# Stage borders of a two-block Hyena/attention network: ScalarE rounds the next input and squares it into the bank just read

## What is computed

```python
y = x32 * lax.rsqrt(jnp.mean(x32 * x32, axis=-1, keepdims=True) + EPS)   # over the 1024 channels
return (y * g.astype(jnp.float32)).astype(x.dtype)
x = x + mixed
x = x + swiglu(rmsnorm(x, norm_ffn[i]), w_gate, w_up, w_down)
```

## Time and profile before

| | us |
|---|---|
| median of 3 runs | 2171.7 (2170.68 to 2172.7) |
| the profiled execution, its own time | 2171.51 |
| its span, first to last instruction | 2169.7 |
| PE busy with matmuls | 2035.8 (94%) |
| DVE busy | 1156.2 (53%) |
| ACT busy | 660.4 (30%) |
| POOL busy | 883.4 (41%) |
| mean granted TensorE clock | 0.941 of full |

### The profile page before, as it was taken

How to read it: one execution, slowest core, us unless ns; L and a number is a source line. 1 busy time by engine, 2 the same in 40 slices (tenths; PEclk the granted TensorE clock), 3 DMA queues, 4 the chain that set the end, 5 groups by cost and what they waited for, 6 DMA issues and landing times. The chain is left out here.

```text
span 2169.7 us, 22805 instructions
## 1 busy us (share of the span) xinstructions
PE 2035.8 (94%) x8683; PEld 1620.5 (75%) x8683; DVE 1156.2 (53%) x1404; ACT 660.4 (30%) x931; POOL 883.4 (41%) x370
## 2 busy tenths in 40 slices
PE   6887788999999999999988999999999969999999
PEld 5665677888888777556866888888787857888887
DVE  6776677544443575544847444433668566535301
ACT  3554432222222223212332322222223342222221
POOL 3465324444454434100531444454443513444442
PEclk8998899999999999657979999999999989999999
DMA  4221012333323322100321333223323303232222
GB/s 145 72 93 58 20 59 78 97 97 97 97 87 107 94 78 79 40 1 20 117 78 39 97 97 97 94 90 97 101 89 116 117 20 96 93 99 92 96 92 73
DMA packets 167194, 179.32 MB, mean 83 GB/s; under 512 B 4511, under 2 KB 156563, under 8 KB 166868
## 3 DMA queue, kind: packets, MB, share of 16 engines
q1 hardware_dynamic: 164036, 172.16, 24.8%
q10 hardware_dynamic: 3088, 6.20, 0.8%
HBM read 176.24 MB, written 2.10 MB: 82 GB/s over the span
## 5 line engine op out<-in xcount | busy, mean ns | idle before, releaser
L1849 POOL TENSOR_TENSOR w_lo<-w_raw,w_hi 128x1024 fp32r<-128x1024 f32 x326 | 817.2, 2527 | 1166.2 <-ACT w_hi L1477 1166.2
L490 PE MATMUL acc<-a_hi,w_hi 128*128 128x512 f32 x1544 | 610.7, 396 | 25.3 <-POOL w_lo L1849 10.9
L491 PE MATMUL acc<-a_lo,w_hi 128*128 128x512 f32 x1544 | 604.7, 392 | 0.0
L492 PE MATMUL acc<-a_hi,w_lo 128*128 128x512 f32 x1544 | 604.4, 391 | 0.0
L1477 ACT ACTIVATE w_hi<-w_raw 128x1024 fp32r<-128x1024 f32 x326 | 327.1, 1051 | 541.9 <-PE acc L492 537.7
L490 PEld LDWEIGHTS acc<-a_hi,w_hi 128*128 128x128 f32 x1544 | 291.8, 189 | 101.0 <-issue 16.0
L491 PEld LDWEIGHTS acc<-a_lo,w_hi 128*128 128x128 f32 x1544 | 291.8, 189 | 62.2 <-issue 1.7
L492 PEld LDWEIGHTS acc<-a_hi,w_lo 128*128 128x128 f32 x1544 | 291.5, 189 | 62.4
L490 PE MATMUL acc<-h_hi,w_hi 128*128 128x512 f32 x528 | 205.4, 389 | 0.0
L491 PE MATMUL acc<-h_lo,w_hi 128*128 128x512 f32 x528 | 205.4, 389 | 0.0
L492 PE MATMUL acc<-h_hi,w_lo 128*128 128x512 f32 x528 | 205.4, 389 | 0.0
(11 more groups left out here) (385 smaller groups left out, 2493.6 us busy)
## 6 DMA issues: line engine op xcount, KB each, us to landing
w_raw<-in_w_gate SPq DMA_DIRECT2D x22, 1024.0 KB, 5.1
w_raw<-in_w_up SPq DMA_DIRECT2D x22, 1024.0 KB, 5.1
w_raw<-in_w_down SPq DMA_DIRECT2D x16, 896.0 KB, 4.8
w_raw<-in_hy_w_in SPq DMA_DIRECT2D x12, 1024.0 KB, 4.9
w_raw<-in_ffn_w_gate SPq DMA_DIRECT2D x11, 1024.0 KB, 5.1
w_raw<-in_ffn_w_up SPq DMA_DIRECT2D x11, 1024.0 KB, 5.1
w_raw<-in_e_w_in SPq DMA_DIRECT2D x10, 1024.0 KB, 5.1
w_raw<-in_xa_wkv SPq DMA_DIRECT2D x8, 1024.0 KB, 5.0
```

Source lines behind the costliest of these rows:

```text
L490: nc.tensor.matmul(o, l_hi, r_hi, start=start, stop=False)
L491: nc.tensor.matmul(o, l_hi, r_lo, start=False, stop=False)
L492: return nc.tensor.matmul(o, l_lo, r_hi, start=False, stop=stop)
L1849: nc.gpsimd.tensor_tensor(w_lo[s][:, half], w_raw[s][:, half], w_hi[s][:, half].bitcast(F32), ALU.subtract)\
```

## The change

On PE, `stats` moves from the end of `o` = 0 to the middle (k = 4) of `o` = 1, and waits for the last bank to be freed in place of a signal on `sumsq`; `key_transposes` loses its wait for `sumsq`. On ACT, `new_x` makes `a_hi` and then writes the square into the PSUM bank of tile k, which DVE has read but not yet freed; `split_next` comes behind it. On DVE, `normed_sum` adds bank k to x and hands over to ACT, adds the square of tile k - 1 from its bank to `sumsq` and only now frees that bank, waits for `a_hi` of tile k, and makes `a_lo`. In the second border the eight tiny products of two gains become one, and the second sum of squares (`tmp`) stays in SBUF.

```diff
@@ wide_block, stats (PE)
-        def wide_block(r_hi, r_lo, kt=KT, outs=2, between=None, wait_from=KT, n=T, rows=P, name=None):
+        def wide_block(r_hi, r_lo, kt=KT, outs=2, between=None, wait_from=KT, n=T, rows=P, name=None,
+                       inside=None):
...
+                    if inside and o == 1 and k == kt // 2:
+                        inside()
...
             if wait:
-                operand()
+                pe.wait_ge(acc_free, n_acc[0] - 2)
...
-            wide_block(a_hi, a_lo, between=stats, wait_from=0)
+            wide_block(a_hi, a_lo, inside=stats, wait_from=0)
...
-        wide_block(a_hi, a_lo, between=even_stats, wait_from=0)
+        wide_block(a_hi, a_lo, inside=even_stats, wait_from=0)
...
             def key_transposes():
-                operand()
@@ DVE
-        def operand(k, gain):
-
-            step(V.tensor_scalar(a_hi[:, k, :], x[:, k, :], gain, None, ALU.mult))
+        def operand_low(k, gain):
+
+            acted()
             for_pe(V.scalar_tensor_tensor(a_lo[:, k, :], x[:, k, :], gain, a_hi[:, k, :].bitcast(F32),
                                           ALU.mult, ALU.subtract))
+
+        def squares_of(k, bank):
+
             acted()
-            add_square(k, sumsq, sq)
+            if k == 0:
+                ins = V.tensor_copy(sumsq[:, :], bank)
+            else:
+                ins = V.tensor_tensor(sumsq[:, :], sumsq[:, :], bank, ALU.add)
+            free_acc(ins, again=True)
...
+        def normed_sum(add, next_gain, after_second=None):
+
+            late = []
             for k in range(KT):
                 bank = take_acc()
-                free_acc(V.tensor_tensor(x[:, k, :], x[:, k, :], bank, ALU.add), again=True)
-                operand(k, par(*next_gain(k)))
+                for_act(add(k, bank))
+                settle()
+                if late:
+                    squares_of(*late.pop())
+                operand_low(k, par(*next_gain(k)))
+                late.append((k, bank))
                 if k == 1 and after_second:
+                    squares_of(*late.pop())
                     after_second()
+            squares_of(*late.pop())
@@ final_residual (DVE), the second border
+            gains = slice(COL["norm_final"], COL["norm_final"] + KT), slice(COL["g_mix_2"], COL["g_mix_2"] + KT)
+            step(V.tensor_tensor(small[:, 80:80 + KT], param[:, gains[0]], param[:, gains[1]], ALU.mult))
...
+                bank = take_acc()
+                for_act(V.tensor_tensor(x[:, k, :], x[:, k, :], bank, ALU.add))
+                settle()
+                if late:
+                    squares_of(*late.pop())
+                    add_square(k - 1, tmp[4], tmp[(k - 1) % 2], last=step)
+                operand_low(k, small[:, 80 + k:81 + k])
+                late.append((k, bank))
@@ ACT
-        def square(k):
-
-            result(S.activation(sq[:, :], x[:, k, :], ACT.Square))
-
-        def residual(blocks=4, per=2, after_second=None):
+        def new_x(k, gain, also=None):
+
+            bank = acc[:, evac.n % 4, :]
+            evac.next()
+            given()
+            result(S.activation(a_hi[:, k, :], x[:, k, :], ACT.Copy, scale=gain))
+            if also:
+                also(k)
+            result(S.activation(bank, x[:, k, :], ACT.Square))
+
+        def residual(gain, blocks=4, per=2, after_second=None):
             for b in range(blocks):
                 for k in range(per * b, per * (b + 1)):
+                    new_x(k, par(*gain(k)))
                     if k == per * (b + 1) - 1:
                         split_next()
-                    evacuated()
-                    square(k)
                     if k == 1 and after_second:
                         after_second()
@@ swiglu (ACT)
                 for k in (2 * pair, 2 * pair + 1):
-                    if k % 2:
-                        split_next()
-                    evacuated()
                     each(k)
+                split_next()
```

More of the change, by code:

```diff
@@ L977, in residual @@
         def residual(next_gain, after_second=None):
+            add = lambda k, bank: V.tensor_tensor(x[:, k, :], x[:, k, :], bank, ALU.add)
+            normed_sum(add, next_gain, after_second)
+        def normed_sum(add, next_gain, after_second=None):
+            late = []
             for k in range(KT):
                 bank = take_acc()
-                free_acc(V.tensor_tensor(x[:, k, :], x[:, k, :], bank, ALU.add), again=True)
-                operand(k, par(*next_gain(k)))
+                for_act(add(k, bank))
[4 more added lines that the diff above has]
+                late.append((k, bank))
                 if k == 1 and after_second:
+                    squares_of(*late.pop())
                     after_second()
+            squares_of(*late.pop())
         step(V.memset(ones[:, :], 1.0))
@@ L1153, in _ @@
         gated_low(1, 3)
[L1154 to L1157, removed]
+        normed_sum(lambda k, bank: V.scalar_tensor_tensor(x[:, k, :], bank, par("hy_b_out", k), x[:, k, :], ALU.add, ALU.add),
+                   lambda k: ("norm_ffn", k))
         def hidden_pair(first):
@@ L1179, in final_residual @@
         def final_residual():
+            gains = slice(COL["norm_final"], COL["norm_final"] + KT), slice(COL["g_mix_2"], COL["g_mix_2"] + KT)
+            step(V.tensor_tensor(small[:, 80:80 + KT], param[:, gains[0]], param[:, gains[1]], ALU.mult))
+            late = []
             for k in range(KT):
[L1183 to L1186, removed]
-                for_pe(V.scalar_tensor_tensor(a_lo[:, k, :], x[:, k, :], gain, a_hi[:, k, :].bitcast(F32),
-                                              ALU.mult, ALU.subtract))
-                acted()
-                add_square(k, tmp[4], tmp[3], last=step)
-                add_square(k, sumsq, sq)
+                bank = take_acc()
[6 more added lines that the diff above has]
+                late.append((k, bank))
+            k, bank = late.pop()
+            acted()
+            add_square(k, tmp[4], tmp[k % 2], last=step)
+            free_acc(V.tensor_tensor(sumsq[:, :], sumsq[:, :], bank, ALU.add), again=True)
         swiglu(final_residual)
@@ L1646, in _ @@
         evac.next(24)
-        residual()
+        residual(lambda k: ("norm_ffn", k))
         def hidden_pair(first):
@@ L1672, in swiglu @@
                 for k in (2 * pair, 2 * pair + 1):
-                    if k % 2:
-                        split_next()
-                    evacuated()
                     each(k)
+                split_next()
         def final_square(k):
-            S.activation(tmp[3][:, :], x[:, k, :], ACT.Square, scale=par("norm_final", k))
-            square(k)
-        swiglu(final_square)
+            S.activation(tmp[k % 2][:, :], x[:, k, :], ACT.Square, scale=par("norm_final", k))
+        swiglu(lambda k: new_x(k, small[:, 80 + k:81 + k], also=final_square))
         for dst, src in ((w_sp[:, :, :], ins["e_w_s_2"][0].rearrange("g t s -> t g s")),
@@ L1753, in _ @@
         load_memory(0)
-        residual(after_second=lambda: memory(0))
+        residual(lambda k: ("g_xa_2", k), after_second=lambda: memory(0))
         def cross(layer):
@@ L1808, in cross @@
                     result(S.activation(xo_hi[:, h, :], aux_bank(("cross", layer, what, h, 0)), ACT.Copy))
-            residual(blocks=2, per=4)
+            residual(lambda k: ("g_ffn_2", 8 * layer + k), blocks=2, per=4)
         cross(0)
-        swiglu(square)
+        swiglu(lambda k: new_x(k, par("g_mix_2", 8 + k)))
         act.dma_start(w_pool[:, :, :], ins["o_w_pool_2"][0].rearrange("g c d -> c g d")).then_inc(in_pool, 16)
@@ L1834, in _ @@
         load_memory(1)
-        residual(after_second=lambda: memory(1))
+        residual(lambda k: ("g_xa_2", 8 + k), after_second=lambda: memory(1))
         cross(1)
-        swiglu(lambda k: None)
+        swiglu(lambda k: evacuated())
     @block.gpsimd
```

## The result

| | before | after |
|---|---|---|
| median, us | 2171.69 (4 runs, 2170.68 to 2172.70) | 2148.32 (4 runs, 2145.08 to 2152.39) |
| the profiled execution, its own time | 2171.51 | 2152.39 |
| its span | 2169.7 | 2150.6 |
| mean granted TensorE clock | 0.941 | 0.946 |

The ratio is 0.9893, interval 0.9872 to 0.9914: faster, as forecast, but by 23.4 us where 17.6 were worked out. The profiled execution, on the other hand, is 2152.39, and the prediction's sum had 2153.9 for it. Both facts need explaining.

A forecast was written before the change was run, and what follows sets the result against it. PE, busy 94% of the span, bounds the kernel, so only its waits can be won: 20.4 us gained at borders less 2.8 lost, net 17.6, gives 2153.9, said as 2154; range 2149.5 to 2162.

The forecast's parts named there:

- reads a bank, so it doesn't wait for POOL: Border sums: DVE's square addition, reading a PSUM bank, escapes POOL's wait; 0.69 us taken, 2.9 from above.
- up to 2 us each: Fourth and seventh border: DVE waits for POOL twice, in tiles 4 and 5, by up to this much.
- DVE's shorter work lets it catch up: Fourth and seventh border: DVE needs 2.3 us per tile, tiles come every 2.7; gain 6.3 us, twice.
- The new waits: Third and sixth border: later rounding makes PE wait for POOL's `w_lo`; cost 1.4 us, twice.
- Given back downstream: Rival, 0.18: even mixer and fifth border lose 3.0 and 1.8 us of the gain again; 2158.7 us.
- Third weight block late: Rival, 0.07: in three SwiGLUs the 0.8 us to spare is used up, each loses 2.5; 2161.4 us.
- Table reloads: Rival, 0.04: scaled copy and square share no ACT function table, two 1.28 us loads per tile; slower, 2177 us.
- How the numbers follow: Closing step, whole kernel: sets chances (0.68 for the forecast, faster 0.91) and bounds 2149.5 to 2157.5, extended to 2162.
- 1.4 more twice: Low bound, third and sixth border: POOL is in time after all, so their new waits vanish; 2151 us.
- 2 for `stats` and columns: Bounds: allowance of 2 us either way for the times taken for `stats` and the second border's columns.

The follow-up runs named there:

- round first: Kernel after, with weight blocks rounded ahead of ACT's two passes again; at the borders 1.3 us slower than the kernel after.
- behind only: Kernel before, with only ACT's rounding moved behind the square; brings 17.2 of the 17.9 us at the borders.
- stats only: Kernel before, with only `stats` moved inside the second tile; first, second and fifth border -1.87, -4.13 and -1.86 us.
- Memory first: Kernel after, with the one rounding ahead of a memory block (third and sixth border) first again; medians 2146.24 and 2152.19 us.

## Why the prediction was right, and where it was wrong

**The two parts of the gain.** Right about where and how much: the profiled execution took 2152.39 where the sum had 2153.9, all the waits for `a_lo` and for `sumsq` at borders are gone, `a_lo` is at 752 ns at the fourth and seventh border's last tile, the last `a_lo` comes 2.8 us into the stage (worked out as 2.7), and the second block ends 22.7 us in (22.8). The step "reads a bank, so it doesn't wait for POOL", the one on which I said that the forecast hangs, holds for all 48 sums. The rule that I set beside it, from the Trainium skill's page "SBUF — State Buffer", section "Who interferes with whom", that whoever of the two issues first holds the shared ports, agrees with the rows here: 2.64 us in "round first" beside POOL, 0.69 for the same work in the kernel after. The trace of the kernel after shows both orders. Of DVE's instructions with two operands in SBUF (`a_lo`, `h_lo`, the products of `tmp` and `rstd`), all 85 that began beside a running `w_lo` ended 0.54 to 0.56 us behind it, and the 35 that began just before one kept their length of at most 0.69. A `w_lo` that began while such an instruction ran took 2.83 us in the median, any other 2.40. So what DVE waits is what is left of POOL's instruction. This is where the prediction's "up to 2 us each" for tiles 4 and 5 was too much: `a_lo` took 1.38 and 1.23 us there, 0.6 and 0.5 over its 0.75, since it begins later in POOL's instruction, behind the addition and the sum from a bank.

Less right was the reason that I gave for the fourth and seventh border, that DVE's shorter work lets it catch up. That cure works ("round first", -6.40), but keeping POOL away works alone too ("behind only", -5.55). They overlap nearly whole: 0.85 us at each of these two need the rest. At the first, second and fifth border there is a third cure, `stats` in the second tile alone ("stats only", -1.87, -4.13 and -1.86). The second border needs rounding behind only with the change's own order of work, in which the second sum of squares stands ahead of the last `a_lo`: in the old order, with rounding ahead, "stats only" gained its 4.13. Whether the new division of work would be enough at the first and fifth without the later `stats` was not run.

**The new waits.** 1.36 for 1.4, in the two halves and at the two borders named. The halves were worked out as 0.3 and 1.2, which makes 1.5 and not the 1.4 of the sum; with what each stop costs behind it they measured 0.4 and 0.95. The list of waits, which was to show entries of 1.4, shows 0.68 each.

**The rivals.** Given back downstream: no. The wait in the even mixer went from 4.99 to 4.7, not to 8, and the fifth border kept 1.85. Third weight block late: no; the fourth and seventh border hold their full 6.4 to the end of the stage, which they could not with 2.5 lost on the way. Table reloads: none beside `new_x`, and the pass took 0.73 us.

**The step that failed** is the one under "How the numbers follow", the bounds of the range: they were made of terms of the borders alone ("1.4 more twice" and "2 for `stats` and columns") around one profiled execution, "against the profiled execution's own 2171.5", as if everything outside the borders would repeat to within nothing. It doesn't. The prediction itself had said that a measurement tells 4.3 us from no change, and left that out of its range. PE's list outside the borders is the same in all kernels, and still these stretches summed to +0.6 us in the kernel before's second execution and to between +0.9 and -6.8 in the others. All 47 runs of the kernel before lie between 2167.76 and 2175.62, where the runs that I had seen lay 2 us apart. The first median of the kernel after came of 2152.39, 2150.84, 2145.80 and 2145.08; the two shortest were at a granted clock of 0.948, the other two at 0.946 and 0.943. The mean clock does not order all its runs, though: later ones took 2151.99 at 0.946 and 2149.96 at 0.943. All twelve runs of the kernel after have a median of 2151.1, inside the range. A term of 3 us to either side for this would have made the low end 2146.5 and held the first median. The bounds don't follow from their own terms either: 2153.9 - 2.8 - 2 is 2149.1, and 2153.9 + 2 is 2155.9, for the 2149.5 and 2157.5 given; the first median is below 2149.1 as well.

What stays: 2171.1 (all runs before) less the borders' 17.9 is 2153.2, and the twelve runs say 2151.1. The odd output projection, 1.3 to 1.6 us shorter in every profiled execution of the kernel after, is no reason for those two, since cross attention 1 takes it back: the two together took 105.9 to 106.0 us in the kernel after and 106.3 and 105.9 in the kernel before. A difference of 2 us I can't tell from scatter.

**Memory first** beats both kernels by its borders (2.7 us below after, shown in two executions each). By its medians it can't be told from after: 2146.24 and 2152.19 against 2148.32, 2151.71 and 2151.10.

## What to carry to other kernels

Before unloading an engine that comes late, ask who stands beside it: here the order of two calls in ScalarE's list, which set when GpSimd began, brought 17.2 of the 17.9 us that the whole change brought at the borders, with no work taken from VectorE, because more than one cure was enough at most of them. Where one moved call serves places with different due times, move it only where it helps: at five borders later rounding was free or needed, at two it cost 1.4 us each. And a range that is made of the change's own terms needs one more, the scatter of what the change doesn't touch; take it from the spread of several timings, and compare kernels by stretches of the trace when the edit is worth less than that.

## What the runs showed of the hardware

The granted clock differs from one execution of a kernel to the next: the same instructions took 160.3 us at 0.65 and 162.1 at 0.64 in the attention, while the borders of the kernel after, which have no long wait, repeated to 0.03 us and those of the kernel before that have one moved by 0.2 to 0.3. Cross attention's 58.4 and 56.05 show a scatter that the mean clock (0.77 and 0.76) does not explain. A wait can cost more than its length: behind the 4.72 us in "stats only" PE ran 6.2 us at the lower clock, and that border was 1.5 us longer than with the same wait in the kernel before, where it ran so for 2.9 us; at the seventh border of "stats only" it was 2.9 us again, and in "round first" 3.1 us behind a wait of 2.25. A DVE instruction with two operands in SBUF that begins beside POOL's 128x1024 subtraction ends 0.55 us behind it; one with an operand in a bank keeps its 0.69. `a_hi`, with one operand in SBUF and none in a bank, waits too (up to 2275 ns for 487 in the kernel before). ScalarE wrote a 128x512 square into a bank in 582 ns, against 632 into SBUF, while the scaled copy that rounds took 725.
